# A first stage by three token tiles beside page gathers, sums of squares by TensorE, and four output slots

## The reference

```python
def rmsnorm(x, g):
    y = xf * lax.rsqrt(jnp.mean(xf * xf, axis=-1, keepdims=True) + EPS)
    return (y * g.astype(jnp.float32)).astype(x.dtype)

def finish(x, m, w_o, g_post_mix, g_pre_ffn, g_post_ffn, w_gate, w_up, w_down):
    x = x + rmsnorm(m @ w_o, g_post_mix)
    h = rmsnorm(x, g_pre_ffn)
    f = (jax.nn.silu(h @ w_gate) * (h @ w_up)) @ w_down
    return x + rmsnorm(f, g_post_ffn)
```

## Time and profile before

| what | value |
|---|---|
| median of 3 runs | 3344.97 us (3344.89 to 3345.18) |
| profiled execution: time / span | 3343.96 us / 3342.2 us |
| PE busy | 3062.3 us, 92% of the span |
| DVE, ACT, POOL busy | 1519.5, 1039.6, 825.1 us |

### The profile page before, as it was taken

How to read it: one execution, slowest core, us unless ns; L and a number is a source line. 1 busy time by engine, 2 the same in 40 slices (tenths; PEclk the granted TensorE clock), 3 DMA queues, 4 the chain that set the end, 5 groups by cost and what they waited for, 6 DMA issues and landing times. The chain is left out here.

```text
span 3342.2 us, 49410 instructions
## 1 busy us (share of the span) xinstructions
PE 3062.3 (92%) x19624; PEld 2673.0 (80%) x19624; DVE 1519.5 (45%) x3358; ACT 1039.6 (31%) x2017; POOL 825.1 (25%) x614
## 2 busy tenths in 40 slices
PE   2999999898899999999769999999899999999994
PEld 2776766658899999999757667565699999999993
DVE  4558776546721121121654785755664211211337
ACT  1336544545411011011222655354442111111121
POOL 4002014115322122243400010313252221223442
PEclk6999999999999999999879999999899999999997
DMA  4110116563211111123211111356412111111223
GB/s 161 41 47 26 39 40 225 177 207 115 65 46 45 45 51 45 45 64 109 69 49 35 42 40 51 142 175 226 165 48 61 45 45 45 51 45 54 64 105 109
DMA packets 256665, 271.95 MB, mean 81 GB/s; under 512 B 25777, under 2 KB 227562, under 8 KB 256298
## 3 DMA queue, kind: packets, MB, share of 16 engines
q1 hardware_dynamic: 234922, 195.27, 18.7%
q0 software_dynamic: 21504, 73.41, 6.5%
HBM read 233.66 MB, written 34.98 MB: 80 GB/s over the span
## 5 line engine op out<-in xcount | busy, mean ns | idle before, releaser
L2009 PE MATMUL ps<-act_hi,w_hi 128*128 128x352 f32 x2112 | 684.0, 324 | 4.3 <-DVE act_lo L2397 3.8
L2009 PE MATMUL ps<-act_lo,w_hi 128*128 128x352 f32 x2112 | 677.0, 321 | 0.0
L2009 PE MATMUL ps<-act_hi,w_lo 128*128 128x352 f32 x2112 | 676.6, 320 | 0.0
L2300 POOL TENSOR_TENSOR w_lo<-w_raw,w_hi 128x1024 fp32r<-128x1024 f32 x132 | 318.1, 2412 | 994.2 <-ACT w_hi L2168 994.1
L678 PE MATMUL ps<-w_in_slots,hT 128*128 128x256 f32 (+3 forms) x2304 | 510.4, 378 | 42.9 <-PEq L185 30.2
L678 PEld LDWEIGHTS ps<-w_in_slots,hT 128*128 128x128 f32 (+1 forms) x2304 | 407.4, 186 | 122.9 <-issue 49.6
L2410 DVE TENSOR_TENSOR a_raw<-ps,silu 128x352 f32<-128x352 f32 x132 | 69.2, 524 | 748.1 <-PE ps L2009 744.2
L2009 PEld LDWEIGHTS ps<-act_hi,w_hi 128*128 128x128 f32 x2112 | 396.2, 188 | 9.6 <-DVE act_lo L2397 5.9
L2009 PEld LDWEIGHTS ps<-act_lo,w_hi 128*128 128x128 f32 x2112 | 396.8, 188 | 0.4
L2009 PEld LDWEIGHTS ps<-act_hi,w_lo 128*128 128x128 f32 x2112 | 396.0, 187 | 0.0
L2009 PE MATMUL ps<-a_hi,w_hi 128*128 128x352 f32 x1056 | 348.8, 330 | 0.0
(11 more groups left out here) (333 smaller groups left out, 4368.3 us busy)
## 6 DMA issues: line engine op xcount, KB each, us to landing
w_raw<-in_w_gate SPq DMA_DIRECT2D x44, 512.0 KB, 3.8
w_raw<-in_w_up SPq DMA_DIRECT2D x44, 512.0 KB, 3.8
w_raw<-in_w_down SPq DMA_DIRECT2D x44, 512.0 KB, 4.0
w_in_slots<-in_w_in SPq DMA_DIRECT2D x19, 1024.0 KB, 5.3
xpark<-xT SPq DMA_DIRECT2D x12, 1408.0 KB, 5.6
xT<-xpark SPq DMA_DIRECT2D x6, 1408.0 KB, 15.3
hT<-xpark SPq DMA_DIRECT2D x6, 1408.0 KB, 15.1
wo_raw<-in_w_o SPq DMA_DIRECT2D x16, 512.0 KB, 5.1
```

The source lines that it names most:

```text
L2009: ins = pe.matmul(bank(b), w, x, start=first and i == 0, stop=end and i == 2)
L2300: pool.tensor_tensor(w_lo[slot(j)][:, 0:K, :], w_raw[slot(j)][:, 0:K, :], w_hi[slot(j)][:, 0:K, :].bitcast(F32), ALU.subtract).then_inc(w_ ...
```

## The change

It has three parts. First, `load_x` and `norm_one` become one block. The page table's rows are worked out first and POOL gathers from then on; x has a slot for each of the nine tiles; turning, squaring, summing and scaling go by three groups of tokens (384, 384 and 288), with copies split over DVE and ACT, and each block's squares go straight into a matmul with ones that accumulates in PSUM. Second, in the last down projection the squares of the new x, and those of f in the last third, are summed by such matmuls too (`take_x`, `take_y`) and no longer added by POOL; the blocks of thirds 1 and 2 rotate over six PSUM banks, and the lists of ACT and DVE are reordered. Third, `store_y` has four slots, eight PSUM banks and copies split over DVE and ACT.

```diff
-        with ExitStack() as st:
-            load_x(c, sem, st)
         early_buffers(c, sem)
-        c.l = 0
         with phase() as st:
-            norm_one(c, st)
+            load_x(c, st)
...
+def load_x(c, st):
...
+    PIECES = ((0, 3), (3, 6), (6, TILES))
+    xt = nc.alloc_sbuf_tensor_at("x_tok", [P, TILES, D], F32, offset=c.m_at)
...
+            sp.dma_start(tables[:, :], io["page_table"].rearrange("b p -> (b p)").rearrange("(o n) -> o n", o=1)).then_inc(table_in, 16)
+            sp.dma_start(page_step[:, :], io["page_step"]).then_inc(table_in, 16)
+            sp.dma_start(c.ident[:, :], io["ident"]).then_inc(ident_in, 16)
+                src = io["x_prompt"][0, n * P:n * P + P, :] if n < PT else io["x_sample"].rearrange("b t d -> (b t) d")
+                sp.dma_start(xt[:tok(n), n, :], src).then_inc(x_in[n], 16)
+            sp.dma_start(g[:, :], gain(io["g_pre_mix"], 0)).then_inc(g_in, 16)
+            load_columns(c, sp, 0, 0)
+            load_columns(c, sp, 1, 0)
+            load_index_constants(c, sp)
+            sp.dma_start(c.rope_h[:, :, :], io["rope_h"].rearrange("p (n w) -> p n w", n=TILES)).then_inc(rope_in, 16)
+            sp.dma_start(c.rope_i[:, :, :], io["rope_i"].rearrange("p (n w) -> p n w", n=TILES)).then_inc(rope_in, 16)
+            for p_, (_, end) in enumerate(PIECES):
+                sp.wait_ge(kept_dve, end)
+                sp.wait_ge(kept_act, end)
+                sp.dma_start(c.xpark.rearrange("p (k t) -> p k t", k=KC)[:, :, at(p_)], xT[:, :, at(p_)]).then_inc(parked, 16)
+            sp.wait_ge(rope_in, 32)
+            sp.wait_ge(parked, 48)
...
+            pool.wait_ge(rows_set, 4)
+            for i in range(DB * PAGES // 4):
+                gather_index_page(c, pool, i, c.page_rows)
...
+            def turn(*tiles):
+                for n in tiles:
+                    m = tok(n)
+                    pe.wait_ge(x_in[n], 16)
...
+            def total(p_):
+                if p_:
+                    pe.wait_ge(rooted, p_)
+                for k in range(KC):
+                    pe.wait_ge(squared, KC * p_ + k + 1)
+                    pe.matmul(ps[:, 6, 0:wide(p_)], c.ones[:, :], sq[:, k % W_SQ, 0:wide(p_)], start=k == 0, stop=k == KC - 1).then_inc(summed, 1)
...
+            pe.wait_ge(ident_in, 16)
+            turn(0, 1, 2, 3)
+            total(0)
+            turn(4, 5, 6)
+            total(1)
+            turn(7, 8)
+            total(2)
...
+            def square(p_):
+                act.wait_ge(kept_dve, PIECES[p_][1])
+                act.wait_ge(kept_act, PIECES[p_][1])
+                for k in range(KC):
+                    if KC * p_ + k >= W_SQ:
+                        act.wait_ge(summed, KC * p_ + k - W_SQ + 1)
+                    act.activation(sq[:, k % W_SQ, 0:wide(p_)], xT[:, k, at(p_)], ACT.Square).then_inc(squared, 1)
+
+            def root(p_):
+                act.wait_ge(summed, KC * p_ + KC)
+                if p_ == 2:
+                    act.wait_ge(h_done, KC)
+                act.activation(rstd[:, p_ % 2, 0:wide(p_)], ps[:, 6, 0:wide(p_)], ACT.Sqrt, bias=c.eps[:, 0:1], scale=1.0 / D).then_inc(rooted, 1)
+
+            keep(0, 1, 2, 3)
+            square(0)
+            root(0)
+            keep(4, 5, 6)
+            square(1)
+            root(1)
+            keep(7, 8)
+            square(2)
+            root(2)
...
+            def first_h(p_):
+                r = rstd[:, p_ % 2, 0:wide(p_)]
+                dve.wait_ge(rooted, p_ + 1)
+                dve.reciprocal(r, r).then_inc(inverted, 1)
+                dve.wait_ge(inverted, p_ + 1)
+                dve.wait_ge(g_in, 16)
+                for k in range(KC):
+                    dve.scalar_tensor_tensor(out=hT[:, k, at(p_)], in0=xT[:, k, at(p_)], scalar=g[:, k:k + 1], in1=r,
+                                             op0=ALU.mult, op1=ALU.mult).then_inc(h_done, 1)
...
+            keep(0, 1, 2, 3, 4)
+            first_h(0)
+            keep(5, 6, 7)
+            first_h(1)
+            keep(8)
+            first_h(2)
...
+    NY = 4
...
+                    if n >= NY:
+                        pe.wait_ge(kept_act if half else kept_dve, n - NY + 1)
...
+        @block.scalar
+        def _(act):
+            for n in range(TILES):
+                m = tok(n)
+                if n >= NY:
+                    act.wait_ge(y_out[n % NY], 16 * (n // NY))
+                act.wait_ge(turned, 2 * n + 2)
+                act.activation(yt[:m, n % NY, 512:1024], ps[:m, (2 * n + 1) % NBANK, :], ACT.Copy).then_inc(kept_act, 1)
...
+
...
                 pe.wait_ge(d_add, (KC - 1) * (th + 1))
-                add_up(acc2[:, :], b, d_sum)
-            def down_sum_2(th, b):
-                pe.wait_ge(x2_add, (KC - 1) * (th + 1))
-                add_up(hT[:, 0, of(th)], b, d_sum)
+                pe.wait_ge(y_done, KC)
+                pe.wait_ge(d_root, th)
+                add_up(acc2[:, :], 6, d_sum)
+            def take_y(d):
+                pe.wait_ge(d_sq, 2 * KC + d + 1)
+                pe.matmul(bank(6), c.ones[:, :], sq2[:, d % 2, :] if d else acc2[:, :], start=d == 0, stop=d == KC - 1).then_inc(d_taken, 1)
+            def take_x(th, *ks):
+                    pe.wait_ge(x2_sq, KC * th + k + 1)
+                    ins = pe.matmul(bank(7), c.ones[:, :], hT[:, k, of(th)], start=k == 0, stop=k == KC - 1)
+                    if k == KC - 1:
+                        ins.then_inc(x2_sum, 1)
...
-                    pe.wait_ge(y_done, KC * (th - 1) + d + 1)
+                    n = KC * (th - 1) + d
+                    pe.wait_ge(y_done, n + 1 if n < 6 else KC + n - 5)
...
-                    if (th, d) == (1, 2):
-                        pe.wait_ge(y_done, KC)
-                        down_sum_1(0, 7)
-                    if (th, d) == (1, 7):
-                        pe.wait_ge(y_done, KC + 6)
-                        down_sum_2(0, 5)
+                    if (th, d) == (1, 1):
+                        sum_y(0)
+                    if (th, d) == (1, 4):
+                        take_x(0, 0, 1)
+                    if (th, d) == (1, 5):
+                        take_x(0, 2, 3, 4)
+                    if (th, d) == (1, 6):
+                        take_x(0, 5, 6, 7)
                     if (th, d) == (2, 0):
-                        pe.wait_ge(y_done, 2 * KC)
-                        down_sum_1(1, 7)
+                        sum_y(1)
+                    if (th, d) == (2, 3):
+                        take_x(1, 0, 1)
+                    if (th, d) == (2, 4):
+                        take_x(1, 2, 3)
                     if (th, d) == (2, 5):
-                        down_sum_2(1, 7)
-            pe.wait_ge(y_done, 2 * KC + 1)
-            down_sum_1(2, 0)
-            down_sum_2(2, 0)
+                        take_x(1, 4, 5)
+                        take_y(0)
+                    if (th, d) == (2, 6):
+                        take_x(1, 6, 7)
+                        for e in range(1, 5):
+                            take_y(e)
+            for e in range(5, KC):
+                take_y(e)
+            take_x(2, *range(KC))
...
-                        act.wait_ge(d_sum, 2 * th - 1)
-                    if d >= 3:
+                        act.wait_ge(d_sum, th)
+                    if th == 2 and d >= 3:
+                        act.wait_ge(d_taken, d - 1)
+                    elif d >= 3:
                         act.wait_ge(d_add, (KC - 1) * th + d - 2)
...
+            square_y(1, 6)
+            root_x(0)
+            square_y(1, 7)
+            root_y(1)
+            square_y(2, 0)
+            square_x2(1, 0, 1)
+            square_y(2, 1)
+            square_x2(1, 2, 3)
+            square_y(2, 2)
+            square_x2(1, 4, 5)
             square_x2(1, 6, 7)
-            square_y(2, 5)
-            root_2(1, 7)
+            square_y(2, 3, 4, 5)
+            root_x(1)
             square_y(2, 6, 7)
-            root_1(2, 0)
+            root_y(2)
             square_x2(2, *range(KC))
-            root_2(2, 0)
+            root_x(2)
...
             add_y2(0, *range(1, KC))
-            add_y2(1, 1, 2, 3)
...
-            add_y2(2, 5, 6, 7)
-            add_x2(2, *range(1, KC))
+            add_y2(1, *range(1, KC))
...
             finish(0, *range(KC))
-            finish(1, 0, 1, 2)
+            finish(1, 0, 1)
             invert_1(0)
-            finish(1, 3)
-            new_x(0, 0, 1)
+            finish(1, 2, 3)
+            new_x(0, 0, 1, 2)
             finish(1, 4)
-            new_x(0, 2, 3, 4)
+            new_x(0, 3, 4)
             finish(1, 5)
             new_x(0, 5, 6, 7)
             finish(1, 6, 7)
             invert_2(0)
             finish(2, 0)
             invert_1(1)
-            next_h(0)
-            finish(2, 1, 2)
-            new_x(1, 0, 1, 2)
-            finish(2, 3)
-            new_x(1, 3, 4, 5)
-            finish(2, 4)
-            new_x(1, 6, 7)
+            new_x(1, 0, 1)
+            finish(2, 1)
+            new_x(1, 2, 3)
```

(9 more changed lines are left out.)

241 lines of the change are left out of this document (84 added, 157 removed).

## The result

| | kernel before | changed kernel |
|---|---|---|
| median of 4 runs each | 3345.07 us (3344.89 to 3346.08) | 3286.45 us (3284.54 to 3289.46) |
| ratio, 95% interval | 1 | 0.9825 [0.9808, 0.9842] |
| profiled execution: time / span | 3343.96 / 3342.2 us | 3287.14 / 3285.4 us |
| granted clock, mean | 0.962 | 0.976 |

The change makes the kernel 58.6 us faster, which is 1.75%; 54 were forecast. To see where they lie I cut both spans at the same events: PE's first projection matmul, the first `finish` of each layer's last down projection, the first projection matmul of the next layer, and the first transpose of y. This table is worked out from the start times of those rows; later ones of the same kind are made the same way.

A forecast was written before the change was run, and what follows sets the result against it. POOL was taken to bound the start, a chain DVE, ACT, POOL, PE each layer's end, the writes the output. Gains 17.5 + 30.4 + 6 = 53.9 take 3343.96 to 3290, median 3291 us; range 3280 to 3302 (0.74).

The forecast's parts named there:

- First stage, forecast 17.5: Start of the kernel up to PE's first projection: PE begins at 61.7 against 79.15 us, gain 17.5, bounds 8 and 25.
- The step from the last engine to PE: End of the first stage: from the last engine's end to PE's first matmul 3.7 us, with 1.1 as the other bound.
- The gathers beside DVE: First stage: POOL's 32 gathers, running beside DVE's work, lose one or two us by the row and end at 49.
- The rival in which the gathers still end the stage: First stage: by the port rule gathers end at 68 us, gain 7.5, time 3301 us; chance 0.05.
- Layer ends, forecast 15.2 each: Last down projection to the next stage, in both layers: gain 15.2 us each, 30.4 together; bounds 17.5 and 9 a layer.
- The four terms: Layer end: gains of 8.6 to block (2,7)'s end, 1.6 to the root of y, 3.9 in `new_x(2)`, 1.1 behind it.
- The order of ACT and DVE: Layer end: their lists make the last `finish` end about 3283.1, not 3280.6; without these 2.5 us the gain is 17.5.
- the rival in which the waits change place: Layer ends: DVE's and ACT's lists are late, PE idles at the insertions, layers give 5 us each, 3311 us; chance 0.12.
- the one in which eleven insertions stall PE: Layer ends: PE stalls at the eleven insertions of sums, slower than before, 3455 us at the full price; chance 0.02.
- Output, forecast 6: Output stage: 14.9 us against 20.9 with overlapping writes of 1.2 us per tile, gain 6, bounds 0 and 8.
- The half-way bounds: Whole kernel: half of each term's bound towards the bad side gives 3308 us, towards the good side 3277.
- The rival "the first stage gives little or nothing": First stage: POOL's first gather is held by something other than the table, no gain there, 3308 us; chance 0.06.

## Why the prediction was right

The time, 3286.45 us against 3291, was near, and each part's mechanism was as described. That the profiled execution is only 2.9 us off its forecast of 3290 is in part luck: the first stage gave 5.35 us more than forecast, and the other terms together 2.45 less.

- *First stage, forecast 17.5, measured 22.85.* The mechanism was right: gathers from 5.72 (6.4 forecast) to 47.13 (49), two pauses, slow sums behind them. Two terms were off. The step from the last engine to PE was taken at 3.7 us with 1.1 as the other bound, because it was "the same place". It measured 0.80: the 3.7 belongs to a stage that ends with gathers, as three profiles show (3.58 to 3.68), and DVE ended this one. That is 2.9 us. And DVE's chain ended at 55.5, not 58.0: its first group was 1.7 us sooner (26.04 against 27.7), mostly since PE turned the first four tiles in 5.70 us and not 6.9, so that ACT's squares began at 12.07 and not 13.6 and the sums ended at 18.07 and not 19.4; the second group added 0.9.
- *The gathers beside DVE.* 32 took 41.4 us, 1.29 each, against 1.33 in the kernel before; the prediction's "one or two" us lost were 1.2. Four of them were stretched, to 1.22 and 1.28 us, two beside the first group's products and two beside the second's. The rival in which the gathers still end the stage (68 us for the last) fell. It rested on the two-port lock of which the Trainium skill tells (SBUF — State Buffer, Who interferes with whom). The prediction found nothing for it in the rows but DVE's slow steps beside POOL's adds, and there the kernel before has more to show:

```profile
35.55 1.26 DVE L1884 TENSOR_TENSOR a_acc<-a_acc,a_sq 128x1056 f32<-128x1056 f32 x1 [3.65 <-ACT a_sq L376]
35.64 2.00 POOL L469 DMA_INDIRECT ki_in<-in_cache_kidx_c,page_rows  x1 [0.30 <-issue]
...
57.46 1.62 POOL L469 DMA_INDIRECT ki_in<-in_cache_kidx_c,page_rows  x1 [0.30 <-issue]
```

  Both gathers end 0.83 us after a DVE instruction with two inputs in SBUF ends (36.80 and 58.25), and so do the six that follow the first of them, at 1.05 to 1.07 us, and the four stretched ones here. So a gather was held, but to the end of the one DVE instruction under way at its start and not for DVE's whole work: 1.04 us behind an add of 1.26, 0.3 behind a product of 0.61. Beside reciprocals, which have one input, none was stretched (0.95 to 0.96 us). That is why the price was small.
- *Layer ends, forecast 15.2 each, measured 14.95 and 14.88.* The four terms stand one by one in the second layer, counted from the first `finish`: up to the end of PE's last block 8.3 us (8.6 forecast), from there to the root of y 1.7 (1.6), `new_x(2)` 3.8 (3.9), the rest 1.05 (1.1). The insertions in thirds 1 and 2 waited 0.44 us in all (0.6 forecast), and 2.06 us stand behind the last block, where the prediction had put the late last `finish`. The order of ACT and DVE, left as a bound, is worth 2.2 to 2.9. With the 0.44 us fell the rival in which the waits change place (3311), and the one in which eleven insertions stall PE.
- *Output, forecast 6, measured 4.3.* The pitch was right (1.22 us against 1.2) and the end was not: 1.2 us were given to the last small tile and the end, and it took 3.7 us from the issue of that write, where it stands behind the overlapping ones. The first write went out at 2.68, as forecast. Nine slots gave nothing, so it is the writes that bound this stage.
- *Sum.* The errors, +5.35, -0.25, -0.3, -1.7 and -0.2 from the bodies, make 2.9: 3287.1 against 3290 for the profiled execution. The range held: the first stage's 22.85 lies inside its bounds of 8 and 25, which came from rows. The half-way bounds are wrongly added up: with half of each term towards its bad or good side the prediction's own numbers give 3305 and 3284, not 3308 and 3277; 3277 is the whole of each.
- *What no step had.* On the third chip the first stage's gain is absent, and on the second the stage took 82 to 84 us with the new code (the kernel before has no profile there). The rival "the first stage gives little or nothing", priced at 3308 and given 0.06, is what they show, though not by its mechanism: the first gather is in time (5.73 us), and DVE and ACT stop behind it.

## What to carry over

When a stage's last engine changes, the step behind it changes too: the time from "last instruction" to "next stage begins" is a property of who ends it (3.6 us for gathers, 0.8 for DVE here), so it is read from a row with the same kind of engine last. An engine that adds up beside a chain of two-input DVE work costs twice, once as a chain and once as a brake; take the two prices apart, since the second falls due wherever the adds run. And a gain that comes from running engines beside POOL's gathers has to be measured on more than one chip.
